# A four-layer encoder trunk: gate and up products by seven block products, down products in six rounds

## The reference

```
def swiglu(x, w1, w3, w2):
    return (jax.nn.silu(x @ w1) * (x @ w3)) @ w2

def half_ffn(x, i, n):
    h = 0.5 * swiglu(x, ffn_w1[i, n], ffn_w3[i, n], ffn_w2[i, n])
    return layer_norm(ALPHA * x + h, ln_g[i, 2 * n], ln_b[i, 2 * n])
```

## Time and profile before

| | |
|---|---|
| median of 3 runs | 2569.51 us (2569.48 to 2569.84) |
| span of the profiled execution | 2569.5 us |
| PE busy | 2544.0 us (99%), 16284 matmuls |
| DVE, ACT, POOL busy | 1107.3, 816.1, 142.8 us |
| DMA | 259.09 MB, 101 GB/s |

### The profile page before, as it was taken

One profiled execution on the slowest core, in us unless ns is written; L12 is line 12 of the kernel. 1 busy time (PEld: TensorE's weight loads), 2 busy tenths in 40 slices (PEclk: granted clock), 3 DMA queues, 4 the chain that ended last, 5 costly groups with the idle time before them and its releaser, 6 DMA issues.

```text
span 2569.5 us, 37727 instructions
## 1 busy us (share of the span) xinstructions
PE 2544.0 (99%) x16284; PEld 2303.6 (90%) x16284; DVE 1107.3 (43%) x1477; ACT 816.1 (32%) x1272; POOL 142.8 (6%) x199
## 2 busy tenths in 40 slices
PE   8999999999999999999999999999999999999998
PEld 8998998899989988899899988777776999899987
DVE  4223323662233236733232261666666732233267
ACT  4222222132222223432122122666665322122133
POOL 3000000100000000000000001222123000000000
PEclk9999999899999999999999999999999999999999
DMA  6213222322132222332232124677776332232121
GB/s 182 73 62 95 72 73 70 107 79 72 62 95 73 71 78 74 96 85 79 62 96 69 62 74 135 192 219 199 218 212 192 97 93 67 62 99 75 53 95 66
DMA packets 376757, 259.09 MB, mean 101 GB/s; under 512 B 10449, under 2 KB 339153, under 8 KB 376592
## 3 DMA queue, kind: packets, MB, share of 16 engines
q1 hardware_dynamic: 371488, 239.64, 32.0%
q0 software_dynamic: 5104, 17.04, 2.0%
HBM read 248.22 MB, written 8.42 MB: 100 GB/s over the span
## 4 chain that ended last, share of the span: by engine, by line
PE 95%; DVE 2%; ACT 1%; issue 1%; DMA 1%; POOL 0%; SPq 0%; DVEq 0%; ACTq 0%
PE ps L1775 86%; PE ps L520 5%; PE ps L552 2%; PE ps L1871 1%; DMA raw<-in_ffn_w_dram 1%; PE ps L628 0%; ACT e_buf L1089 0%; ACT wt L1114 0%; DVE ring L1376 0%; ACT kc_t L1073 0%; DVE x L1420 0%; DVE s_sum L1539 0%; DVE x L1428 0%; DVE e_buf L1504 0%; PE ps L543 0%
## 5 line engine op out<-in xcount | busy, mean ns | idle before, releaser
L1775 PE MATMUL ps<-xt_hi,ring 128*128 128x256 f32 (+1 forms) x6160 | 1340.0, 309 | 4.0 <-ACT xt_hi L1050 2.3
L1775 PEld LDWEIGHTS ps<-xt_hi,ring 128*128 128x128 f32 x6160 | 1035.9, 190 | 12.7 <-issue 9.6
L1775 PE MATMUL ps<-xt_lo,ring 128*128 128x384 f32 (+1 forms) x3080 | 944.7, 309 | 0.0
L1775 PEld LDWEIGHTS ps<-xt_lo,ring 128*128 128x128 f32 x3080 | 583.8, 190 | 0.2
L1775 PE MATMUL ps<-ring,h_hi 128*128 128x512 f32 x1760 | 550.0, 392 | 0.0
L1030 ACT ACTIVATE ring<-raw 128x1024 fp32r<-128x1024 f32 x326 | 324.8, 1029 | 428.3 <-PE ps L1775 351.7
L1376 DVE TENSOR_TENSOR ring<-raw,ring 128x1024 fp32r<-128x1024 f32 x326 | 383.3, 1204 | 137.2 <-ACT ring L1030 132.8
L1775 PEld LDWEIGHTS ps<-ring,h_hi 128*128 128x128 f32 x1760 | 332.7, 189 | 68.9
L1638 DVE SCALAR_TENSOR_TENSOR act<-act,ps 128x384 f32<-128x384 f32 (+1 forms) x176 | 85.8, 488 | 667.3 <-PE ps L1775 667.3
L1775 PE MATMUL ps<-ring,h_lo 128*128 128x512 f32 x880 | 344.2, 391 | 0.0
L1264 ACT ACTIVATE h_hi<-act 128x384 fp32r<-128x384 f32 (+1 forms) x176 | 83.0, 472 | 626.4 <-DVE act L1638 626.4
(11 more groups left out here) (137 smaller groups left out, 1606.0 us busy)
## 6 DMA issues: line engine op xcount, KB each, us to landing
raw<-in_ffn_w_dram SPq DMA_DIRECT2D x256, 512.0 KB, 4.4
k_raw<-in_cache_k_dram SPq DMA_DIRECT2D x128, 256.0 KB, 4.8
v_raw<-in_cache_v_dram SPq DMA_DIRECT2D x128, 256.0 KB, 4.3
raw<-in_sb_w_in_dram SPq DMA_DIRECT2D x24, 512.0 KB, 5.8
raw<-in_ple_w_gate_dram SPq DMA_DIRECT2D x16, 512.0 KB, 4.7
g_b<-in_ln_g_dram POOLq DMA_DIRECT2D x8, 512.0 KB, 4.2
b_b<-in_ln_b_dram POOLq DMA_DIRECT2D x8, 512.0 KB, 5.9
raw<-in_ffn_w_dram SPq DMA_DIRECT2D x16, 256.0 KB, 3.4
```

Of the source, the lines that this page charges most:

```text
L1775: return pe.matmul(out, w, xx, start=first, stop=last, skip_group_check=True)
```

## The change

The feed-forward block is one stage ("ffn") of 22 chunks. The matrix product [gate | up] of one chunk is taken as a product of 2 x 2 blocks: tokens in two halves of 320 (the fifth tile is shared between them, 64 columns each), D_MODEL in two halves of 512, and columns in gate and up. It is formed from seven block products of 320 columns, 12 matmuls each (`product1` to `product7`). Their operands are the blocks themselves and sums and differences of blocks:

- of the weights, once a chunk: DVE forms two differences in one instruction (`first_diffs`), GpSimd two more (`diffs`), into t_buf. A chunk is now 3.5 units to split (A, B, D and half a unit C) instead of two.
- of x, once a block: for two tiles in DVE's and GpSimd's `pair_sums`, for the fifth tile in GpSimd's `quarter_of`; the sums are transposed as `S12a`, `S43a`, `S12b`, `S43b`, and half tiles as `X22a`, `X22b`: 40 transposes in the first products of a block.

Some products go on in the bank of another without starting it anew; between, ACT copies partial sums out (`c1`, `r_sum`, `c5`), and DVE adds them. The down products run in six rounds (`ROUNDS`: 2 chunks, then five times 4), behind chunks 2, 6, 10, 14, 18 and the last, with 6 or 12 matmuls an output, three banks, and an addition to x each time. In the last round the two halves of a tile follow each other, and tiles are normalised there. The fifth tile's part of each hidden chunk is rounded and split on GpSimd (`hidden_quarter`). The loop over `range(3, FC)` at the end of the excerpt is ACT's. The fifth tile now comes first in most stages (`ORDER`), the band matrices are built behind the first block's last chunk, as their place in SBUF is taken until then, and ring slots are given out by hand ("a" to "g").

```diff
-FH = FC // 2
+HT = TOKENS // 2
+HC = DC // 2
+HK = HC * P
+ROUNDS = ((0, 2), (2, 4), (6, 4), (10, 4), (14, 4), (18, 4))
+ORDER = (4, 0, 1, 2, 3)
+GATE_UP = (0, 2, 3)
+GATE_BANK = 1
+UP_BANK = 4
...
+            def block_product(bank, u, col, x_hi, x_lo, first):
+                for c in range(HC):
+                    for hl, xx in ((0, x_hi), (0, x_lo), (1, x_hi)):
+                        ins = mm(ps[:, bank, 0:HT], ring[:, slot, hl, col + c * P:col + (c + 1) * P], xx[:, c, :],
+                                 first and c == 0 and hl == 0 and xx is x_hi, c == HC - 1 and hl == 1)
+            def product3(st, q):
+                if q == 0:
+                    pe.wait_ge(piece_lo, st.prev.piece["S43b"][0])
+                split_of(u)
+                pe.wait_ge(c5_done, n + 1)
+                block_product(UP_BANK, u, items[u].col, *s4_op, False).then_inc(p3_full, 1)
+            def product4(st, q):
+                pe.wait_ge(up2_done, n + 1)
+                block_product(up_bank(q), u, HK, *x22, False).then_inc(p4_full, 1)
+            def period(st, q):
+                product1(st, q)
+                product2(st, q)
+                product7(st, q - 1)
+                product5(st, q)
+                product6(st, q)
+                product4(st, q - 1)
+                product3(st, q)
...
+            def diffs(st, q):
+                pool.wait_ge(t13_done, n + 1)
+                pool.tensor_tensor(t_buf[:, 1, :], raw_of(("up", st, q))[:, HK:], t_buf[:, 0, :],
+                                   ALU.subtract).then_inc(t24_done, 1)
+                pool.wait_ge(t24_done, 2 * n + 1)
+                pool.tensor_tensor(t_buf[:, 3, :], raw_of(("gate", st, q))[:, HK:], t_buf[:, 1, :],
+                                   ALU.subtract).then_inc(t24_done, 1)
+            def hidden_quarter(st, q):
+                pool.wait_ge(h1_done, n + 1)
+                pool.wait_ge(h2_done, n + 1)
+                pool.tensor_copy(hidden_parts(0, i)[1], act_parts(q)[1]).then_inc(h4_done, 1)
+                pool.wait_ge(h4_done, 2 * n + 1)
+                pool.tensor_tensor(hidden_parts(1, i)[1], act_parts(q)[1], hidden_parts(0, i)[1].bitcast(F32),
+                                   ALU.subtract).then_inc(h4_done, 1)
...
+                for q in range(3, FC):
+                    cvt_to(unit["D", q] + 1)
+                    first_product(st, q)
+                    cvt_to(unit["A", q + 1] + 1 if r is None else unit["U", (r, 0)] + 1)
+                    if r is None:
+                        cvt_to(unit["C", q + 1] + 1)
+                    silu_of_first(st, q)
+                    cvt_to(unit["B", q + 1] + 1 if r is None else unit["U", (r, 1)] + 1)
+                    fifth_product(st, q)
+                    common_sum(st, q)
+                    if r is not None:
+                        cvt_to(unit["U", (r, 2)] + 1)
+                    silu_of_second(st, q - 1)
+                    hidden_hi(st, q - 1)
+                    if r is not None:
+                        cvt_to(unit["U", (r, 3)] + 1)
```

More of the change, by code:

```diff
@@ L106, in number_events, with __init__ @@
     return order, table
+BLOCK_PIECES = (("x0", 4), ("x1", 6), ("x2", 4), ("S12a", 6), ("X22a", 5), ("S43a", 6), ("S12b", 4), ("S43b", 6),
+                ("X22b", 5))
+TILE_PIECES = (("x0", 4), ("x1", 6), ("x2", 4), ("x3", 6), ("x4", 4))
+INPUT_PIECES = (("p0", 6), ("p1", 4))
 class Stage:
-    def __init__(self, kind, layer, n=0, half=0, ln=None, then="none"):
-        self.kind, self.layer, self.n, self.half = kind, layer, n, half
-        self.ln, self.then = ln, then
-        self.head = False
-        self.part0 = self.y0 = self.gate0 = self.norm0 = self.piece0 = self.free0 = self.u0 = 0
-        self.prev = None
+    def __init__(self, kind, layer, n=0, ln=None, then="none", halves=True):
+        self.kind, self.layer, self.n = kind, layer, n
+        self.ln, self.then, self.halves = ln, then, halves
+        self.y0 = self.gate0 = self.norm0 = self.free0 = self.u0 = self.q0 = self.f = 0
+        self.piece = {}
+        self.item = {}
+        self.prev = self.next = None
     @property
     def per_dh(self):
-        return {"down": 6, "embed": 5, "out": 4, "v": 4}[self.kind]
-    def order(self):
-        steps = [(p, i) for i in range(FH) for p in range(2)]
-        if self.head:
-            steps[:4] = [(0, 0), (0, 1), (1, 0), (1, 1)]
-        return steps
-    def part_at(self, p, i):
-        return self.part0 + self.order().index((p, i)) + 1
-    def piece_at(self, t):
-        return self.piece0 + t + 1
-LATE = ('pool',)
+        return {"embed": 5, "out": 4, "v": 4}[self.kind]
+Item = namedtuple("Item", "kind stage at slot col cols load")
 def plan_stages():
-    stages = [Stage("load", 0, then="split")]
+    stages = [Stage("load", 0, then="blocks")]
     for layer in range(DEPTH):
@@ L147, in plan_stages @@
         for n in range(2):
[L148 to L151 removed]
+            stages.append(Stage("ffn", layer, n, ln=2 * n))
             if n == 0:
@@ L162, in plan_stages, with add_pieces @@
-    part = y = gate = norm = piece = free = units = 0
+                stages.append(Stage("embed", layer, ln=3, then="none" if layer == DEPTH - 1 else "blocks"))
+    y = gate = norm = free = pieces = ffns = 0
+    on_bank = {}
+    def add_pieces(st, names):
+        nonlocal pieces
+        for name, bank in names:
+            pieces += 1
+            wide = 1 if name.startswith("X22") else 2
+            before = max(on_bank.get(b, 0) for b in range(bank, bank + wide))
+            for b in range(bank, bank + wide):
+                on_bank[b] = pieces
+            st.piece[name] = (pieces, bank, before)
@@ L163, in plan_stages @@
     for st, before in zip(stages, [None] + stages[:-1]):
-        st.part0, st.y0, st.gate0, st.norm0, st.free0, st.u0 = part, y, gate, norm, free, units
+        st.y0, st.gate0, st.norm0, st.free0 = y, gate, norm, free
         st.prev = before
-        if st.kind == "embed":
-            st.pt0 = piece
-            piece += PLE // P
-        st.piece0 = piece
-        if st.kind == "gu":
-            st.head = before.then != "none"
-            part += 2 * FH
-            units += 2 * FH
-        if st.kind in ("down", "out", "embed"):
+        if before is not None:
+            before.next = st
@@ new lines, in streaming_trunk @@
+        slot_free = {}
+        holders = {}
+        for u, item in enumerate(items):
+            waits = []
+            for col in range(item.col, item.col + item.cols, HK):
+                before = holders.get((item.slot, col))
+                if before is not None and freed[before] not in waits:
+                    waits.append(freed[before])
+                holders[item.slot, col] = u
+            if item.stage.kind == "out":
+                if item.slot == SLOT["c"] and item.at < 4:
+                    waits = [(z_full, NU * PAIRS)]
+                elif item.slot == SLOT["d"]:
+                    waits = [(s_full, NU * PAIRS - 2)]
+                elif item.slot in (SLOT["e"], SLOT["f"], SLOT["g"]):
+                    waits = [(pv_done, NU * PAIRS), (k_stored, 32 * PAIRS)]
+            slot_free[u] = waits
@@ L1706, in _ @@
                     add_bias(TILES)
+                    if st.then == "blocks":
+                        first_diffs(st.next, 0)
                     for t in range(TILES):
@@ L1744, in _ @@
                     normalise(st, 0)
+                    cvt_to(unit["A", 1] + 1)
+                    first_diffs(st.next, 0)
                     mix(1)
```

1532 lines of the change are left out of this document (1048 added, 484 removed).

## The result

| | before | changed |
|---|---|---|
| median | 2569.20 us (11 runs, 2567.23 to 2571.03) | 2574.11 us (11 runs, 2571.47 to 2575.95) |
| ratio to before | | 1.0018, 95% interval 1.0010 to 1.0026 |
| span of the profiled execution | 2569.5 us | 2569.7 us |

A forecast was written before the change was run, and what follows sets the result against it. It took columns through TensorE as the bound. A gain of 135.3 us less losses of 47.2, 14.2, 17.6, 16.0, 10.0, 8.0 and 5.0 left 17.3 us faster: 2552 us, range 2495 to 2605.

The forecast's parts named there:

- step 4: Down-product rounds: TensorE waits 1.1 us for the low part of h, 16 times, 17.6 us lost.
- P7 and P4 of the last chunk: End of each block: two products left over from the heads, 1.78 us each, 14.2 us lost in four blocks.
- Step 1: Gate and up products: 84 matmuls of 320 columns at 148.1 ns instead of 96, saving 1.78 us a chunk.
- Step 2: Steady chunks: DVE busy 8.8 of 12.4 us, no TensorE wait, 2.3 us spare before product 4; 135.3 us gained.
- The slower rival: Steady chunks: GpSimd stretches DVE's 8.8 us to 10 to 11.2, delaying the up sum; 2620 us, chance 0.11.
- Step 3: First three chunks of each block: more transposes and waits for operands lose 47.2 us; leftover products at the end 14.2.
- Steps 5 to 7: Last rounds 16 us lost, bands 10, clock 8, contention 5.
- The last round: End of each block, where tiles are normalised: TensorE's waits lose 4.0 us a block, 16 in all.
- The bands' wait: First windowed turn waits 12 us for GpSimd's band matrices, partly covering other lag; 10 us lost once (0 to 15).
- the separate 8: Clock lowered behind idle stretches in the heads and bands: 8 us lost, between 0 and 17.
- Contention: GpSimd stretching DVE in the heads, and one more load before the embed stage's second half: 5 us lost (0 to 12).
- heads cost what they gain: Each wait of the heads and rounds a third longer, 25 us more: 2577 us, chance 0.09.

The follow-up runs named there:

- E7: Changed kernel with ScalarE copying P5 and P6 of chunk 0 ahead of the rounding of B of chunk 1 in each block's head: 2572.32 us, ratio 1.0016.
- E9: Changed kernel with ScalarE rounding the fifth tile's four sums behind the third norm's statistics instead of the fourth's in the embed stage: 2572.49 us, ratio 1.0013.
- E1: Changed kernel with VectorE forming the low part of h ahead of the split of the round's fourth weight unit: 2549.83 us, ratio 0.9923.
- E2: Changed kernel with each round's first three outputs taking all chunks but the last, then the last chunk for each: 2546.09 us, ratio 0.9909.
- E4: Changed kernel with GpSimd's twelve subtractions for the band matrices made one instruction of 1536 columns: 2567.31 us, ratio 0.9994.
- E3: Changed kernel with the fifth tile's part of each hidden chunk rounded on ScalarE and split on VectorE instead of GpSimd: 2585.87 us, ratio 1.0063.

## Why the prediction was wrong, by its own steps

It had the direction wrong. Its gain of 135 us and its costs of 118 lie 17 apart, and the costs came out 15 us higher and the gain 2 lower. The step that failed is step 4, the rounds: 30.0 us where 17.6 were put. That is 12.4 of the 22 us between 2552 and 2574. The heads and the chunks make 6.8, the other terms give back 1.4, and 4.7 lie outside the profiled executions.

The table sets the terms of the sum against the same pieces of the two profiled executions. A head runs from the last matmul of the stage ahead to the first of the round behind chunk 2 (before: to the end of chunk 2, by 14.07 us a chunk back from the first down stage).

| step | predicted | measured | how |
|---|---|---|---|
| 1, 2: 76 steady chunks | -135.3 | -133 | 76 x (14.07 - 12.32) |
| 3: four heads | +47.2 | +51.7 | 20.3, 13.3, 11.3, 6.8 |
| 3: P7 and P4 of the last chunk | +14.2 | +14.1 | 8 x 1.76 |
| 4: rounds | +17.6 | +30.0 | 16 x 1.39 + 4 x 1.94 |
| 5, 6, 7: last round, bands, clock, contention | +39.0 | +37.7 | 10.9 last rounds of three blocks; 18.2 from the end of the first block's last P7 to the end of the pool stage, P4 taken off; 5.9 embed, 1.8 attention and out, 0.9 last stage |
| sum | -17.3 | +0.5 (spans: +0.2) | rounding of the rows |

- **Step 1 was right.** 146.6 ns a matmul where 148.1 was read between the rows of 384 and 256; both kernels' chunks are a little cheaper than worked out (12.32 and 14.07 for 12.44 and 14.22), and the saving is 1.75 for 1.78. By the formula that the Trainium skill (TensorE: Matmul & The Clock Gate, "Back-to-back issue gap") gives for a lone matmul, the estimate was 1.63, some 9 us less over the 76 chunks: here its difference falls short, as the rows of before had suggested.
- **Step 2 was right in its result, with less to spare than it had.** TensorE has no idle time in 48 us. But VectorE's full chunk is 9.80 us, not 8.8: beside GpSimd's differences the split of A takes 2.14 us and that of C 1.39, where 1.2 and 0.7 were put in, though the earlier trace rows had shown the stretching. So the up sum is ready at 7.3 on the period's clock instead of 6.6 (1252.53 in a chunk that starts at 1245.28), and P4, due at 8.8, has 1.5 us to spare instead of 2.3. The slower rival (VectorE as the bound, 10 to 11.2 us a chunk) was near in VectorE's time. It fell by its own counter-argument, that only part of the row lies ahead of the up sum.
- **Step 3 was nearly right as a sum (51.7 for 47.2), by errors that partly cancel.** Head by head it had 23.3, 6.7, 11.6 and 5.6, and 20.3, 13.3, 11.3 and 6.8 were measured. In the third head P5 was to start 21.7 us behind the embed stage's last matmul, and does at 21.6; P3 waits 3.4 us for 4.3, P1 of chunk 2 2.3 for 2.4. The second head's 6.6 us too few are mostly a slip in the baseline: before's second head was put at 575.8 us as if it were like the third, while its piece of the earlier trace rows has 24 matmuls fewer behind 541.51 (2619 for 2643) and its three chunks end at 571.1. What the reading missed is what E7 and E9 showed in the third head: taking out one wait there made another as long.
- **Step 4 failed.** Its mechanism is right: the row h_lo, 15.6 on the period's clock, is the wait of 1.07 that was forecast as 1.1. Its size is wrong in two ways. "Four times a block" leaves out the round behind chunk 2, where only the first chunk's matmuls stand ahead of the second chunk's low part: 1.94 us, four times, 7.8. And a wait of 1.07 costs 1.39 between the matmuls around it: 16 x 0.3 = 4.8. E1 gave back 24 us and E2 28, which their timelines account for (24.3 and 27.3). A reader should count a stall by the distance of the matmuls around it.
- **Steps 5 to 7 were right as a sum (37.7 for 39.0), and that is luck.** The last round loses 3.6 us a block for 4.0. The bands' wait is 15.8 for 12: the building takes 24.6 us (450.4 to 475.0) where the walk had 21.7. The wait and what it hides of the last round and the clock come to 18.2 together. The clock's loss rose by 20.6 us, but most of this is inside the heads (17.8) and already in their measure, so the separate 8 was mostly counted twice, and hides the bands and the contention that were put too low. Contention was put at 5: 8.6 were lost, 5.9 of it in the embed stage, where ScalarE waits for the load of A of chunk 1; 2.6 of these are the clock, which E7's profile does not have.

So the change gains 133 us in the profiled execution and pays as much. The case "heads cost what they gain" (2577, 0.09) is the nearest in number. Its point, heads and rounds a third dearer, is near what happened: they cost 81.7 us together where 64.8 were put, a quarter more. But it meets 2577 only with the 4.7 us outside the profiles, of which it says nothing.

Left open are these 4.7 us. The runs of the changed kernel spread over 4.5 us and those of before over 3.8. In the profiled executions of the experiments the clock's loss in the first head was 2.9 to 7.6 us wherever TensorE idled there, and 0.0 in the three that filled its waits. That would be enough for the spread, and in E7 the slowest run (2579.61 us) has a mean clock of 0.976 and the fastest (2569.20) one of 0.982. In the changed kernel's own runs time and clock hardly go together (0.980 in the fastest, 0.979 in the slowest, 0.984 in the one next to the fastest), so it isn't shown.

## What to carry to other kernels

A cheaper algorithm on the bounding engine pays only where it runs in a steady state: here an eighth of the gate and up products' matmuls was saved and spent again, in the profiled executions wholly, on operands that have to be formed first (the heads), on the split of one long stage into rounds, and on a clock that falls when TensorE waits. Before such a change goes in, count every boundary that it makes, with the distance of the matmuls around it and not with the idle time alone, and move independent matmuls ahead of the newest operand: that alone turned 0.2% slower into 0.9% faster. A wait that disappears says nothing until the one behind it on the same chain has been looked at.

## What the runs showed of the hardware

- A wait of 1.07 us for one operand cost 1.39 us between the matmuls around it, and the first matmul behind lasted 0.50 us where the others last 0.39.
- The granted clock was 0.50 in the five microseconds around the end of an idle stretch of 3.7 us (1060 to 1065). At the same place, behind a wait of 3.4 us, it was 0.50 in E4's profile and 1.00 in E7's. So one profile more or less with a lowered clock, some 2.6 us here, says nothing of an edit.
- The clock was 1.00 in the windows of the first head when its waits were filled with transposes that nobody reads; the filling of all four heads gave 8 us.
- In E3 it fell behind a wait of 1.9 us, and the matmuls of 512 columns stood 0.43 us apart instead of 0.23.
- On GpSimd twelve subtractions of 128 columns took 8.75 us and one of 1536 columns 4.24.
- VectorE's split of 1024 rose from 1230 to 1437 ns in the mean (2.14 us for the one beside GpSimd's differences), and GpSimd's second difference took 1848 ns where the first took 1296. In the steady part TensorE waited for neither.
